# Sixteen pieces of w_mod: from TensorE's matrix-vector products to ScalarE's multiplies and GpSimd's sums

## The reference, cut to what matters

```
def adaln(cvec, w_mod, b_mod):
    m = jax.nn.silu(cvec) @ w_mod + b_mod
    return jnp.split(m, 6, axis=-1)

sh1, sc1, gt1, sh2, sc2, gt2 = adaln(c, w_mod, b_mod)
csh1, csc1, cgt1, csh2, csc2, cgt2 = adaln(c_ctx, w_mod, b_mod)
hl = modulate(xl, g_mix, sh1, sc1)
hc = modulate(xc, g_mix, csh1, csc1)
```

## Time and profile before

| | |
|---|---|
| time, median of 3 runs | 2343.03 us (2342.55 to 2343.63) |
| the profiled execution | 2344.29 us, its span 2342.9 us, mean granted clock 0.933 |
| PE busy | 2001.8 us (85%) |
| DVE busy | 959.4 us (41%) |
| ACT busy | 731.6 us (31%) |
| POOL busy | 42.5 us (2%) |
| DMA | 672.10 MB, mean 287 GB/s |
| chain that ended last | PE 49%, DMA 34%, DVE 11%, ACT 4% |

### The profile page before, as it was taken

The page is one execution under the profiler, slowest core; times in us unless marked ns, Lnnn a source line. Parts: engine busy times, 40 slices in busy tenths (PEclk is TensorE's granted clock), DMA queues, the critical chain, the costliest instruction groups (busy, mean ns, idle before and its releaser), DMA issues.

```text
span 2342.9 us, 29605 instructions
## 1 busy us (share of the span) xinstructions
PE 2001.8 (85%) x12486; PEld 1353.7 (58%) x12486; DVE 959.4 (41%) x1623; ACT 731.6 (31%) x1190; POOL 42.5 (2%) x47
## 2 busy tenths in 40 slices
PE   6999778777777778777778789989999899999997
PEld 3556413333333433332444389968999899785786
DVE  3534422122122212212533254567664645653486
ACT  4322221011011111112210053454654544543365
POOL 0000000000000000000000000000000000000010
PEclk9989889899999899898889999999999999999999
DMA  9967899999999999999999965535345555250430
GB/s 395 419 239 272 327 421 418 413 413 413 414 415 416 413 414 417 409 414 408 413 408 410 410 206 180 181 105 162 118 134 182 163 173 186 88 208 19 144 117 19
DMA packets 210436, 672.10 MB, mean 287 GB/s; under 512 B 11504, under 2 KB 134512, under 8 KB 152192
## 3 DMA queue, kind: packets, MB, share of 16 engines
q1 hardware_dynamic: 210304, 670.21, 74.3%
HBM read 669.12 MB, written 1.05 MB: 286 GB/s over the span
## 4 chain that ended last, share of the span: by engine, by line
PE 49%; DMA 34%; DVE 11%; ACT 4%; issue 2%; SPq 0%; POOL 0%; DVEq 0%; ACTq 0%; POOLq 0%
DMA ring<-in_w 24%; PE pb L231 11%; PE pb L232 11%; PE pb L233 11%; DMA ring<-in_w_a 6%; DVE WB L329 3%; DMA ring<-in_w_in 3%; PE pb L1775 3%; PE pb L1799 2%; PE pb L770 2%; ACT WB L323 1%; DMA ring<-in_w_mod 1%; PE pb L994 1%; PE pb L964 1%; PE pb L3053 1%
## 5 line engine op out<-in xcount | busy, mean ns | idle before, releaser
L329 DVE TENSOR_TENSOR WB<-ring,WB 128x1024 fp32r<-128x1024 f32 (+3 forms) x370 | 426.3, 1194 | 521.9 <-ACT WB L323 521.5
L323 ACT ACTIVATE WB<-ring 128x1024 fp32r<-128x1024 f32 (+3 forms) x370 | 361.8, 1027 | 814.1 <-DMA ring<-in_w_a 461.6
L231 PE MATMUL pb<-HH,WB 128*128 128x256 f32 (+1 forms) x1680 | 495.6, 295 | 11.4 <-DVE WB L329 4.3
L232 PE MATMUL pb<-HL,WB 128*128 128x256 f32 (+1 forms) x1680 | 484.8, 289 | 0.0
L233 PE MATMUL pb<-HH,WB 128*128 128x256 f32 (+1 forms) x1680 | 484.0, 288 | 0.0
L1775 PE MATMUL pb<-ring,big 128*32 128x512 f32 x2048 | 295.9, 669 | 144.5 <-DMA ring<-in_w 128.0
L231 PEld LDWEIGHTS pb<-HH,WB 128*128 128x128 f32 x1680 | 331.5, 197 | 37.3 <-issue 22.6
L232 PEld LDWEIGHTS pb<-HL,WB 128*128 128x128 f32 x1680 | 331.6, 197 | 2.5 <-issue 2.3
L233 PEld LDWEIGHTS pb<-HH,WB 128*128 128x128 f32 x1680 | 331.1, 197 | 0.0
L1775 PEld LDWEIGHTS pb<-ring,big 128*32 128x32 f32 x2048 | 46.4, 112 | 358.3 <-DMA ring<-in_w 268.8
L1799 PE MATMUL pb<-ring,big 128*32 128x512 f32 x1024 | 170.1, 655 | 54.8 <-DMA ring<-in_w 46.8
(11 more groups left out here) (450 smaller groups left out, 1954.7 us busy)
## 6 DMA issues: line engine op xcount, KB each, us to landing
ring<-in_w SPq DMA_DIRECT2D x384, 1024.0 KB, 16.5
ring<-in_w_a SPq DMA_DIRECT2D x66, 1024.0 KB, 13.1
ring<-in_w_in SPq DMA_DIRECT2D x38, 1024.0 KB, 9.9
ring<-in_w_ada SPq DMA_DIRECT2D x36, 1024.0 KB, 6.7
ring<-in_w_b SPq DMA_DIRECT2D x33, 1024.0 KB, 5.0
ring<-in_w_mod SPq DMA_DIRECT2D x24, 1024.0 KB, 11.1
ring<-in_w_out SPq DMA_DIRECT2D x8, 1024.0 KB, 5.0
ring<-in_b_w_in SPq DMA_DIRECT2D x8, 1024.0 KB, 6.4
```

The costliest lines, as they stand in the source:

```text
L231: pe.matmul(o, l[0], r[0], start=start, stop=False)
L232: pe.matmul(o, l[0], r[1], start=False, stop=False)
L323: act.activation(WB[:, c % 2, 0, x:y], flat[:, x:y], ACT.Copy).then_inc(*A(("high", c, z)))
L329: dve.tensor_tensor(WB[:, c % 2, 1, x:y], flat[:, x:y], WB[:, c % 2, 0, x:y].bitcast(F32), ALU.subtract).then_inc(*V(("low", c, z), *([("f ...
```

## The change

The 16 units of `MOD[1]` and `MOD[2]`, of which only `c`'s vector is used, leave PE's matrix-vector products. ACT multiplies each loaded unit by the 128 values of silu(`c`) of its rows, in place (for u = 0 into `acc`, which is `X[:, 2:4]`, now free for longer); POOL adds units 1 to 7 to `acc`, in four pieces of 512 columns each; PE then sums over the partitions with 16 matmuls against a column of ones, and DVE adds the bias. POOL's last addition frees the slot. `g2` now holds only the `ADA` groups, and the units per round are set by lists. `MOD[1]`'s sums come with the pick of `ADA[0]`, `MOD[2]`'s with that of `ADA[2]`. The load of `ctx_2` moves behind `MOD[2]`'s sums.

```diff
+    acc = X[:, 2:4, :].rearrange("p a b -> p (a b)")
+    SUMS = {ADA[0]: MOD[1], ADA[2]: MOD[2]}
+    def sp_products(sp, v):
+        for u in range(8):
+            load(sp, (v, u), I["w_mod"][0][128 * u:128 * u + 128, 2048 * v[1]:2048 * v[1] + 2048], 2048)
+            yield
+    def act_products(act, v):
+        for u in range(8):
+            act.wait_ge(*landed((v, u)))
...
+            elif u == 0:
+                act.wait_ge(*at("sums", MOD[1]))
+            act.activation(slot((v, u)) if u else acc, slot((v, u)), ACT.Copy, scale=cs_lat(u)).then_inc(
+                *A(("product", v, u), *([] if u else [("free", (v, u))])))
+            yield
+    def pool_products(pool, v):
+        pool.wait_ge(*at("product", v, 0))
+        for u in range(1, 8):
+            pool.wait_ge(*at("product", v, u))
+            for j in range(4):
+                x = slice(512 * j, 512 * j + 512)
+                if u > 1:
+                    pool.wait_ge(*at("partial", v, u - 1, j))
+                pool.tensor_tensor(acc[:, x], slot((v, u))[:, x], acc[:, x], ALU.add).then_inc(
+                    *G(("partial", v, u, j), *([("free", (v, u))] if j == 3 else []), ...))
+    def pe_sums(pe, v, bank):
+        pe.wait_ge(*at("products", v))
+        for i in range(16):
+            e = pe.matmul(bank[:, 32 + i:33 + i], acc[:, 128 * i:128 * i + 128], ones[:, 0:1], start=True, stop=True)
+        e.then_inc(*P(("sums", v)))
+    def dve_sums(dve, v, bank):
+        dve.wait_ge(*at("sums", v))
+        dve.tensor_tensor(mcol1[:, c:c + 16, 0], bank[:, 32:48], col("b_mod", c, 16), ALU.add)...
@@ pe_gemv, pick and before the next group
             pe.wait_ge(*at("mraw", v))
+            if v in SUMS:
+                pe_sums(pe, SUMS[v], gemv_bank(v))
...
+                if owed[-1] in SUMS:
+                    pe.wait_ge(*at("mcol", SUMS[owed[-1]]))
@@ units per round; on all engines steps(g2, 3) becomes steps(g2, G_UNITS[q]) and so on
+    G_UNITS, H_UNITS = (0, 1, 1, 1, 2, 2, 1, 2), (2, 2, 1, 2, 1, 2, 1, 1)
+    M1_UNITS, M2_UNITS = (0, 3, 2, 2, 1, 0, 0, 0), (1, 1, 0, 0, 1, 1, 1, 1, 1, 1, 0, 0)
@@ sp_first
-        g2 = sp_gemv(sp, MOD[1:] + ADA)
+        g2, m1, m2 = sp_gemv(sp, ADA), sp_products(sp, MOD[1]), sp_products(sp, MOD[2])
         for q in range(8):
-            if q == 1:
-                sp.wait_ge(*at("xn", "h1", 2))
-                sp.wait_ge(*at("xn", "h1", 3))
-                sp.dma_start(X[:, 2:4, :], I["ctx_2"]...).then_inc(once["ctx_2"], 16)
             if q == 4:
                 load(sp, "gains", I["rows"][:, 0:1152], 1152, hold=True)
             load_chunk(sp, q + 1)
             if q:
-                steps(g2, 3)
+                units_of(m1, M1_UNITS[q])
+                steps(g2, G_UNITS[q])
@@ score products (SP, PE, ACT, DVE)
-            steps(g2, 2)
+            units_of(m2, M2_UNITS[n])        # SP and ACT
+            steps(g2, 1)
@@ heads
-            steps(g2, 2)
+            units_of(m2, M2_UNITS[4 + h])    # SP and ACT
+            steps(g2, H_UNITS[h])
@@ sp_experts
         steps(g2, 8)
+        sp.wait_ge(*at("sums", MOD[2]))
+        sp.dma_start(X[:, 2:4, :], I["ctx_2"]...).then_inc(once["ctx_2"], 16)
@@ pool_program
+        pool_products(pool, MOD[1])
+        pool_products(pool, MOD[2])
         pool.wait_ge(*at("xh"))
```

More of the change, by code:

```diff
@@ L119, in steps, with units_of @@
             break
+def units_of(g, n):
+    for _ in range(n):
+        next(g, None)
 def run(g):
@@ L741, in sp_gemv, with cs_lat @@
                 yield u + 1 == gemv_units(v)
+    acc = X[:, 2:4, :].rearrange("p a b -> p (a b)")
+    SUMS = {ADA[0]: MOD[1], ADA[2]: MOD[2]}
+    def cs_lat(u):
+        return cs_flat[:, 2 * u:2 * u + 1]
+    def sp_products(sp, v):
[5 more added lines that the diff above has]
+            act.wait_ge(*landed((v, u)))
+            if u == 0 and v == MOD[1]:
+                act.wait_ge(*at("xn", "h1", 2))
+                act.wait_ge(*at("xn", "h1", 3))
+            elif u == 0:
[12 more added lines that the diff above has]
+                pool.tensor_tensor(acc[:, x], slot((v, u))[:, x], acc[:, x], ALU.add).then_inc(
+                    *G(("partial", v, u, j), *([("free", (v, u))] if j == 3 else []), *([("products", v)] if u == 7 and j == 3 else [])))
+    def pe_sums(pe, v, bank):
[4 more added lines that the diff above has]
+    def dve_sums(dve, v, bank):
+        c = 16 * v[1]
+        dve.wait_ge(*at("sums", v))
+        dve.tensor_tensor(mcol1[:, c:c + 16, 0], bank[:, 32:48], col("b_mod", c, 16), ALU.add).then_inc(*V(("mcol", v)))
     def pe_gemv(pe, group, waits):
@@ L760, in pe_gemv @@
                 pick(owed[-1])
-                pe.wait_ge(*at("mcol", owed.pop()))
+                pe.wait_ge(*at("mcol", owed[-1]))
+                if owed[-1] in SUMS:
+                    pe.wait_ge(*at("mcol", SUMS[owed[-1]]))
+                owed.pop()
             for w in waits.get(v, ()):
@@ L906, in pe_first @@
         turn(2)
-        g2 = pe_gemv(pe, MOD[1:] + ADA, {MOD[1]: [("turned", "h1", 7, 1)], ADA[0]: [("qkv_out", 0)]})
+        g2 = pe_gemv(pe, ADA, {ADA[0]: [("turned", "h1", 7, 1)]})
         for q in range(4):
@@ L951, in pe_first @@
             e.then_inc(*P(("used", 4 + q), *([("gm",)] if q == 3 else [])))
-            steps(g2, 3)
+            steps(g2, G_UNITS[4 + q])
             if q:
@@ L1086, in act_first @@
                 sp_.upto(kk // 2)
-        g2 = act_gemv(act, MOD[1:] + ADA, MOD[0])
+        g2, m1, m2 = act_gemv(act, ADA, MOD[0]), act_products(act, MOD[1]), act_products(act, MOD[2])
         for q in range(4):
             sp_.upto(q + 1)
+            units_of(m1, M1_UNITS[q])
             if q:
-                steps(g2, 3)
+                steps(g2, G_UNITS[q])
         act.wait_ge(*at("qkv"))
@@ L1105, in act_first @@
             sp_.upto(5 + q)
-            steps(g2, 3)
+            units_of(m1, M1_UNITS[4 + q])
+            steps(g2, G_UNITS[4 + q])
             act_root(act, ("qk", q), st[:, 16:16 + (10 if q < 2 else 2)], [("qk_sums", q)], 1.0 / 64)
@@ L1114, in act_first @@
         for n in range(4):
-            steps(g2, 2)
+            units_of(m2, M2_UNITS[n])
+            steps(g2, 1)
         run(act_row(act, "gt", gt1, 5))
@@ L1148, in act_first @@
                 weights(h + 1)
-            steps(g2, 2)
+            units_of(m2, M2_UNITS[4 + h])
+            steps(g2, H_UNITS[h])
             steps(gg, 1)
@@ L1189, in dve_first @@
                 sp_.upto(p)
-        g2 = dve_gemv(dve, MOD[1:] + ADA)
+        g2 = dve_gemv(dve, ADA)
         for q in range(4):
@@ L1682, in sp_experts @@
         steps(g2, 8)
+        sp.wait_ge(*at("sums", MOD[2]))
+        sp.dma_start(X[:, 2:4, :], I["ctx_2"].rearrange("a (t p) d -> p (a t) d", p=128)).then_inc(once["ctx_2"], 16)
         load(sp, "router", I["w_router"][0].rearrange("(a p) n -> p a n", p=128), 128, "p (a n) -> p a n", a=8)
```

3 lines of the change are left out of this document (2 added, 1 removed).

## The result

| | before | after |
|---|---|---|
| time, median | 2343.33 us (2342.55 to 2343.66, 4 runs) | 2399.26 us (2396.63 to 2401.44, 4 runs) |
| ratio, 95% interval | | 1.0239 [1.0221, 1.0256] |
| the profiled execution | 2344.29 us, span 2342.9 | 2396.63 us, span 2395.3 |
| mean granted clock | 0.933 | 0.911 |
| POOL busy | 42.5 us | 119.9 us |

The account below looks back on a forecast made before the run. It took PE, DMA and DVE, within a tenth of each other, to bound the first block, whose delay reaches the end one to one. 2344.29 + 16 = 2360.3, less 1.26 for the median: 2359.0 us; range 2343 to 2369.

Parts of the forecast that it names:

- Step 1: First block: ACT multiplies three units first, so chunk c3, split at 53.55 before, is split at 57.7; POOL starts at 55.7.
- Steps 2 and 3: First block: slots free later, so chunk c5, issued at 56.59 before, goes out at 74.6; ACT's q copies begin at 76.6.
- Step 4: First block: POOL works to about 101; DVE's norms and rotary embedding end at 103 instead of 87.05, +16 us.
- the turns: DVE instructions reading two SBUF operands alternate with POOL's additions, each waiting about 1.1 us.
- Step 5: Norms' end to first score product: 26.8 us instead of 23.9; scores start at 129.8, +18.9.
- Step 6: Score products: 3 units and a pick fewer on PE, -4.0 us, leaving +14.9.
- Step 7: Heads: 4 units fewer -3.7, MOD[2]'s sums +3.8, POOL's late sum +0.5, gating +0.7; +16 in all.
- Deeper: Rival: ACT's multiplies delay exponentials, DVE pays on PSUM too, clock falls; half these sums on top, 2367 us; chance 13%.
- The clock term: PE's clock may fall in new stalls, mostly ahead of waits that hide a slow PE: 0 to 4 us.
- the expected saving of 9.6 us: PE: 14.8 us of units and 2.5 of picks go, 7.7 of sums are added, if PE stays the bound.
- the rival that drew on it: PE stays the bound, with POOL and ring keeping ahead of it: 9.6 us saved, 2333.4 us; chance 13%.

Follow-up runs that it names:

- with pairs: The changed kernel with two units after each four score products instead of one, and two, none, two, none in the heads: 2386.77 us.
- with wide sums: The changed kernel with each of PE's 32 sum matmuls moving 128 equal columns of ones instead of one: 2387.66 us.
- with both: The changed kernel with units two at a time between score products and in every other head, and 128-column sum matmuls: 2372.47 us.
- the one-column multiply: The changed kernel with paired units, 128-column sums, POOL's additions cut to one a group, and ACT's multiply one column wide except u = 0: 2342.55 us.
- no work on POOL: The changed kernel with paired units, 128-column sums, slots freed by ACT's multiply and POOL's additions left out but one a group: 2352.63 us.
- The two halves: The changed kernel with only MOD[1] moved and MOD[2] on PE again: 2366.97 us; with only MOD[2] moved and MOD[1] on PE: 2365.4 us.
- the last experiment: The kernel before, with PE's two units ahead of each four score products, and the first head's two ahead of both heads' transposed scores: 2349.92 us.
- the kernel with lone units: The kernel before, with one unit after each four score products instead of two, and the units so moved placed in the heads: 2352.42 us.

## Why the prediction was wrong in size

**What held.** Steps 1 to 5, to within 2 us at the marks below but two, which came 4 us early. Step 1: c3 split at 56.4 (57.7 forecast), POOL starts 54.8 (55.7). Steps 2 and 3: c5 issued 73.1 (74.6), ACT's copies of q at 75.0 (76.6), which start behind the multiply of m6. Step 4: norms done at 99.0 (103), POOL at 97.2 (101); the turns cost 0.9 to 1.1 us each in the rows above. Step 5: first score at 128.5 (129.8), its sums 3.57 us (3.8). SP waited 106.5 us for POOL over the first 330 us, PE 16.3 us for loads between 60 and 102. The closeness at the end is partly luck: the kernels with pairs, with wide sums and with both share this stage with after but for the width of the sums, and their first scores came at 133.06, 132.98 and 126.79.

**Step 6 failed: "Score products: 3 units and a pick fewer, -4.0".** It came to +8.2 (33.9 us for 25.75). The term was not mis-sized as work: with every record at the duration that it has at granted clock 1.00, after's loop is 33.9 - 15.7 = 18.2 us (four groups of scores that lost 1.5 and three times 3.5, four units 0.93 each) and before's is 25.75 - 3.5 = 22.3, a difference of -4.1. What was missing is the clock. The row products behind it add 2.4.

**Step 7 failed: "Heads: ... +16" in all, +1.3 by its terms.** It came to +26.5 (88.1 us for 61.65). The work of 188 to 201 and 228 to 262 us, at 0.50 instead of 1.00, is some 21 of it. The rest: PE waits 3.9 us (0.8 before) for the exponentials and the gating behind ACT's multiply, as the rival "Deeper" had it, and 3.2 us for loads of `w_ada`. The second group's sums are 6.92 us, not 3.8.

**The clock term, "0 to 4 us", was the error.** I had looked for new stalls in the rounds only. The clock was lost in the sums, where PE had no stall at all (granted 0.60 from 120 to 122 us), and in the first scores, just behind waits of 0.94 and 0.37 us that before has too; before lost it there as well, and the change had taken away the pair that brought it back. In the heads it was lost behind new waits: 3.9 us at 184 to 188, behind ACT's multiply, and 1.25 and 1.06 us for loads at 224 to 228 (waits of 1.26, 0.52 and 1.42 us for loads did not cost it in the kernel with wide sums). Pairs and wide sums together gave back 26.8 us, the one-column multiply 10.1.

**Where the expected saving of 9.6 us went.** "If PE stays the bound" was the condition, and the rival that drew on it looked at PE's 39.4 of 40 us. The DMA share in the same rows was 1.02 and 1.01. With no work on POOL PE is 6 us less busy and nothing is earlier. So in the rounds PE's relief was worth nothing even without POOL's work. In the heads, where the DMA is not full (share 0.70 from 140 to 206 us before), it was worth up to 6.9 us of the stage (61.7 to 54.8 with the one-column multiply), of which the median shows nothing clear of noise.

**The account.** In this order: pairs and wide sums 2399.3 to 2372.5 (26.8); POOL's additions and their hold on the ring, to 2352.6 (19.8); ACT's multiply, to 2342.6 (10.1). That is 56.7 us for the 55.9 measured; the 0.8 that is over is what PE's saving is worth at the end, and it is within the noise: the one-column kernel's interval runs from 4.0 us faster than before to 0.7 slower. The order matters by 7 us: with POOL's work taken away first it is worth 26.8, and pairs and wide sums then 19.9. The two halves measured apart, 23.5 for `MOD[1]` and 21.9 for `MOD[2]`, make 45.4, and the kernel with both, in pairs, lost 43.2.

**What stays open.** Why a pair restores the clock at one place (116.69 before, 138.97 in pairs) and not at another (184.25 with wide sums, 142.88 in the last experiment) no run settles. The place where it is lost varies between executions: before lost it in the first score products, the kernel with lone units, the same up to there, did not. Each profile is one sample of it. So is the first score after the change: 126.79 to 133.06 us in four profiles of nearly the same work, so that stage differences of a few us between two profiles say little. How turns and ring share POOL's 20 to 27 us is not split. No version run here beats before.

## What to carry to other kernels

Where PE and the DMA were both full, work taken off PE bought nothing, and a ring slot that a slower engine frees is charged to every load behind it. An engine's busy time is not the cost of putting it to work: ask in front of which urgent instruction its new work queues, and which operands it takes turns on. When light PE work is thinned out or split into single pieces, look at the granted clock by stretch: here regrouping the units and widening the sums gave back 20 to 27 us, by the order in which one takes things away, as much as all of POOL's work.

## What the runs showed of the hardware

- A POOL memset of 128x2048 f32 took 1.87 us and left DVE's two-operand instructions at 1.83 and 2.36 us; an addition beside them made these 4.08 and 4.39.
- POOL's addition of 128x512 f32 took 1.23 us from two tiles and 1.01 with the same tile as both inputs.
- 16 f32 matmuls (32 records) against 128x128 stationary pieces took 3.73 us with one moving column and 3.73 with 128 at granted clock 1.00, 6.96 at 0.50. The loads of the pieces were busy for all of 3.55 us from 124.25 us on in the kernel with wide sums, so I read the time as theirs.
- Both granted clock levels held through a loop of score products and lone units: 0.50 from 131 to 162 us in after, 1.00 from 111 to 129 in the kernel before with lone units.
